# Six recurrence levels as 64x64 products on two output halves, gathered in a 512-column table

## The reference

```python
def hgrn2_recurrence(q, k, v, logf):       # 4 heads, key and value width 128
    n = T // CHUNK                          # CHUNK = 64, so 4 chunks
    def step(S, blk):
        G = jnp.cumsum(gc, axis=-2)
        decay = jnp.exp(jnp.where(causal, G[t] - G[s], MASK_VALUE))
        scores = jnp.einsum('bhtd,bhsd,bhtsd->bhts', qc, kc, decay)
        o = scores @ vc + (qc * jnp.exp(G)) @ S
        S = S * jnp.exp(G_end) + (kc * jnp.exp(G_end - G)).T @ vc
        ...
```

## Time and profile before

| | |
|---|---|
| median of three runs | 796.02 us (795.48 to 796.18) |
| profiled execution | 795.0 us, of which the span of the instructions is 793.2 us |
| PE busy | 784.6 us, 99% |
| DVE busy | 585.7 us, 74% |
| ACT busy | 479.5 us, 60% |
| POOL busy | 28.0 us, 4% |
| DMA | 149.55 MB, mean 189 GB/s |

### The profile page before, as it was taken

How to read it: one execution, slowest core, us unless ns; L and a number is a source line. 1 busy time by engine, 2 the same in 40 slices (tenths; PEclk the granted TensorE clock), 3 DMA queues, 4 the chain that set the end, 5 groups by cost and what they waited for, 6 DMA issues and landing times.

```text
span 793.2 us, 11382 instructions
## 1 busy us (share of the span) xinstructions
PE 784.6 (99%) x4440; PEld 672.9 (85%) x4440; DVE 585.7 (74%) x682; ACT 479.5 (60%) x582; POOL 28.0 (4%) x63
## 2 busy tenths in 40 slices
PE   8999999999999999999999999999999999999998
PEld 8988888888998987888888998888888888888877
DVE  7799885576678888557558678458589878686883
ACT  6875487544676558653467654444477666665682
POOL 8100000000000000300000000000000000000000
PEclk9999999999999999999999999999999999999999
DMA  8555344465436624456636435664049979797921
GB/s 273 187 180 163 127 137 159 160 212 177 142 115 204 196 86 145 138 197 193 209 113 206 161 108 170 204 208 159 1 153 344 370 281 336 264 324 257 348 83 53
DMA packets 70037, 149.55 MB, mean 189 GB/s; under 512 B 8458, under 2 KB 11104, under 8 KB 69984
## 3 DMA queue, kind: packets, MB, share of 16 engines
q1 hardware_dynamic: 69568, 148.78, 55.4%
q0 software_dynamic: 384, 0.04, 0.2%
q10 hardware_dynamic: 32, 0.01, 0.0%
HBM read 147.76 MB, written 1.05 MB: 188 GB/s over the span
## 4 chain that ended last, share of the span: by engine, by line
PE 89%; DVE 4%; ACT 3%; DMA 2%; issue 1%; SPq 1%; POOL 0%; POOLq 0%; DVEq 0%; ACTq 0%
PE mm L613 16%; PE mm L615 16%; PE mm L614 16%; PE aux L1107 5%; PE aux L1109 5%; PE aux L1108 5%; PE mm L629 3%; PE mm L630 3%; PE mm L631 3%; PE aux L721 3%; PE aux L835 2%; DMA sb_raw<-in_w_in 2%; PE aux L613 1%; PE aux L615 1%; PE aux L614 1%
## 5 line engine op out<-in xcount | busy, mean ns | idle before, releaser
L1691 DVE TENSOR_TENSOR sb_w_lo<-sb_raw,sb_w_hi 128x2048 fp32r<-128x2048 f32 (+2 forms) x153 | 319.4, 2097 | 74.2 <-ACT sb_w_hi L1223 40.7
L1223 ACT ACTIVATE sb_w_hi<-sb_raw 128x2048 fp32r<-128x2048 f32 (+1 forms) x83 | 155.1, 1871 | 118.3 <-PE mm L615 87.6
L613 PE MATMUL mm<-sb_w_hi,sb_hT_hi 128*128 128x512 f32 (+1 forms) x456 | 175.8, 386 | 0.6 <-DVE sb_w_lo L1691 0.5
L615 PE MATMUL mm<-sb_w_hi,sb_hT_lo 128*128 128x512 f32 (+1 forms) x456 | 172.6, 379 | 0.0
L614 PE MATMUL mm<-sb_w_lo,sb_hT_hi 128*128 128x512 f32 (+1 forms) x456 | 172.6, 379 | 0.0
L1539 ACT ACTIVATE sb_w_hi<-sb_raw 128x2048 fp32r<-128x2048 f32 x50 | 95.6, 1917 | 35.7 <-PE aux L1109 17.7
L613 PEld LDWEIGHTS mm<-sb_w_hi,sb_hT_hi 128*128 128x128 f32 x456 | 85.8, 188 | 18.2 <-issue 2.8
L615 PEld LDWEIGHTS mm<-sb_w_hi,sb_hT_lo 128*128 128x128 f32 x456 | 85.8, 188 | 16.2
L614 PEld LDWEIGHTS mm<-sb_w_lo,sb_hT_hi 128*128 128x128 f32 x456 | 85.9, 188 | 15.0
L629 PE MATMUL mm<-sb_hT_hi,sb_w_hi 128*128 128x256 f32 x272 | 78.2, 288 | 0.0
L630 PE MATMUL mm<-sb_hT_lo,sb_w_hi 128*128 128x256 f32 x272 | 76.9, 283 | 0.0
(11 more groups left out here) (395 smaller groups left out, 1183.2 us busy)
## 6 DMA issues: line engine op xcount, KB each, us to landing
sb_raw<-in_w_in SPq DMA_DIRECT2D x120, 512.0 KB, 4.6
sb_raw<-in_w_down SPq DMA_DIRECT2D x32, 512.0 KB, 5.4
sb_raw<-in_w_gate SPq DMA_DIRECT2D x31, 512.0 KB, 4.7
sb_raw<-in_w_up SPq DMA_DIRECT2D x31, 512.0 KB, 6.1
sb_raw<-in_w_out SPq DMA_DIRECT2D x16, 512.0 KB, 4.1
sb_raw<-in_w_up_attn SPq DMA_DIRECT2D x8, 512.0 KB, 4.6
sb_raw<-in_w_up_hgrn SPq DMA_DIRECT2D x8, 512.0 KB, 4.0
sb_raw<-in_w_o SPq DMA_DIRECT2D x8, 512.0 KB, 4.1
```

What stands on the lines that cost most here:

```text
L613: pe.matmul(dst, a_hi, rhs[0], start=start, stop=False, skip_group_check=True)
L615: return pe.matmul(dst, a_lo, rhs[0], start=False, stop=stop, skip_group_check=True)
L1223: act.activation(w_hi[:, slot(t), 0:width], raw[:, slot(t), 0:width], ACT.Copy).then_inc(hi_split, 1)
L1691: return dve.tensor_tensor(out_, a, b, op)
```

## The change

The pair level and levels 2 to 6 have groups of at most 64 tokens. So each block of 128 tokens is now cut in two stretches of 64. For each of the eight blocks, TensorE does two products with 64 columns of weights and 64 moving columns over all 128 rows: one for the lower half, whose output goes to PSUM partitions 0 to 63, and one for the upper half, whose output goes to partitions 64 to 127, both in the same 64 columns. The 96 products of 128x128x128 become 192 of 128x64x64, the halves in turn.

The result of a level is 128 x 512 and not 128 x 1024. `take_level` gathers it with masks of 64 columns in a new table `near` of 512 columns. When level 6 is in, ScalarE copies `near` to the two diagonal quadrants of each block of `acc` in two instructions of 64 partitions x 512 columns (`spread_near`, in step 15 behind `level_exp(8)` and ahead of `exps(2)`). TensorE's `hgrn_out` waits for both of them too, and in the second layer VectorE's first `take_level` waits for the first layer's copies. Level 7, level 8 and the rest stay. In the setup there are six masks of 128x64 in place of seven of 128x128, and one more table of 512 columns is filled with zeros.

```diff
-N_MASKS = len(LEVELS) - 1
+N_MASKS = len(LEVELS) - 2
...
-        lmask = sb("lmask", [P, len(LEVELS) - 1, P], U8)
+        lmask = sb("lmask", [P, N_MASKS, 64], U8)
+        near = sb("near", [P, 512])
...
                         a, b = (fT, logf) if j == "pair" else (e, e)
                         for i in range(8):
-                            last = pe.matmul(ps[:, i * P:(i + 1) * P], a[:, i * P:(i + 1) * P], b[:, i * P:(i + 1) * P],
-                                             start=True, stop=True)
+                            for h in range(2):
+                                block = slice(i * P + 64 * h, i * P + 64 * h + 64)
+                                last = pe.matmul(ps[64 * h:64 * h + 64, i * 64:(i + 1) * 64], a[:, block], b[:, block],
+                                                 start=True, stop=True, skip_group_check=True)
...
                 def hgrn_out():
                     pe.wait_ge(S["acc_ready"], L + 1)
+                    pe.wait_ge(S["near_spread"], 2 * L + 2)
...
+                def spread_near():
+
+                    act.wait_ge(S["near_ready"], L + 1)
+                    for h in range(2):
+                        rows_ = slice(64 * h, 64 * h + 64)
+                        act.activation(acc[rows_, :].rearrange("p (i t) -> p i t", i=8)[:, :, rows_],
+                                       near[rows_, :].rearrange("p (i t) -> p i t", i=8), ACT.Copy).then_inc(S["near_spread"], 1)
...
-                    15: [lambda: level_exp(8), lambda: exps(2, L, 4), lambda: sink_exp(2, 4)],
+                    15: [lambda: level_exp(8), spread_near, lambda: exps(2, L, 4), lambda: sink_exp(2, 4)],
...
-                for i, j in enumerate(LEVELS[:-1]):
+                for i, j in enumerate(LEVELS[:-2]):
                     size = 1 if j == "pair" else 1 << (j - 1)
-                    ins = dve.tensor_scalar(begins_i[:, i:i + 1], iota_s[:, i:i + 1], -size, None, ALU.bitwise_and)
+                    ins = dve.tensor_scalar(begins_i[:, i:i + 1], iota_s[:, i:i + 1], 64 - size, None, ALU.bitwise_and)
...
-                    ins = ts_(lmask[:, i, :], iota_f, begins[:, i:i + 1], ALU.is_ge)
+                    ins = ts_(lmask[:, i, :], iota_f[:, 0:64], begins[:, i:i + 1], ALU.is_ge)
...
             link(dve.memset(acc[:], 0.0))
+            link(dve.memset(near[:], 0.0))
...
-                    ins = dve.copy_predicated(acc[:, :].rearrange("p (i t) -> p i t", i=8),
-                                              lmask[:, LEVELS.index(j):LEVELS.index(j) + 1, :].broadcast_to([P, 8, P]),
-                                              aux[pair][:, :].rearrange("p (i t) -> p i t", i=8))
-                    release(ins, aux_free[pair], value)
+                    if j == "pair" and L == 1:
+                        dve.wait_ge(S["near_spread"], 2)
+                    ins = dve.copy_predicated(near[:, :].rearrange("p (i t) -> p i t", i=8),
+                                              lmask[:, LEVELS.index(j):LEVELS.index(j) + 1, :].broadcast_to([P, 8, 64]),
+                                              aux[pair][:, 0:W].rearrange("p (i t) -> p i t", i=8))
+                    release(ins, aux_free[pair], value, S["near_ready"] if j == 6 else None)
```

More of the change, by code:

```diff
@@ L368, in build @@
                  "fT_ready", "sig_ready", "log_ready", "kTh_ready", "qTh_ready",
-                 "vh_ready", "D_ready", "k_taken", "q_taken", "E_ready", "W_ready", "acc_ready", "sc128_ready",
+                 "vh_ready", "D_ready", "k_taken", "q_taken", "E_ready", "W_ready", "acc_ready", "near_ready", "near_spread", "sc128_ready",
                  "qk_ready", "v_ready", "qT_ready", "kT_ready", "S_ready", "p_ready", "p_normed", "z_scaled", "sinkexp_in",
```

## The result

The changed kernel takes 787.79 us, the median of four runs (787.30 to 788.18). The kernel before, run beside it, took 795.75 us (795.45 to 796.18). The profiled execution took 787.45 us (span 785.7 us) against 795.0 us: 7.55 us less.

The account below looks back on a forecast made before the run. TensorE's list of work, busy 99% of the span, was taken to bound the kernel. Savings of 2.83 and 4.08 us took 6.9 off 795.0, giving 788.1; 1.0 more for the median made 789.1 us, range 787.9 to 792.0.

Parts of the forecast that it names:

- The saving between the levels and the experts: Both layers' levels, pair to 6: shorter products and masked copies save 2.83 and 4.08 us, 6.9 us together.
- Blocks of products: TensorE, levels pair to 6: two halves go as one, so a block takes 1.42 us where it took 2.02.
- the change of width: TensorE, going to half-width products: 0.09 us added ahead of each new block, between 0 and 0.11 at level 5.
- Rival A: TensorE's levels: halves run in turn, a block grows to 2.35 us, kernel slower at 797.9 us; chance 0.07.
- Masked copy: VectorE, 12 copies: 512 columns take 0.74 us where 1024 took 1.325, 0.585 us less each.
- Levels 3 to 6: First layer: 0.97, 0.70, 0.65 and 0.51 us saved, sum 2.83; second layer, with pair and level 2, 4.08.
- Rival B: VectorE: the masked copy does not get shorter, so only 4.4 us are saved, 791.6 us; chance 0.12.
- Spread: ScalarE's two copies, at most 2.0 us, fit its 2.47 us idle before the third attention unit's exponentials: no cost.
- Rival C, the clock: First layer, after pair and level 2: idle TensorE falls to 1.2 GHz for 3 us stretches; about 792 us; chance 0.05.
- 0 saved: First layer, pair: the next tile waits for VectorE's low part until 49.79 us, so shorter products gain nothing there.
- Nothing is given back: From 82 us on no TensorE product waits for VectorE, so none of the saving is lost later: 0 us.
- the median of three lies 1.0 above it: Last step, whole kernel: 1.0 us added to the profiled execution's 788.1, giving 789.1 us.

Follow-up runs that it names:

- experiment 5: Changed kernel with each level's eight lower-half products issued first, then all eight upper ones, instead of alternating: 794.86 us.
- experiments 3: Changed kernel with every masked copy on VectorE done twice in a row, products still in halves: 791.92 us.
- number 4: Changed kernel with the old 128x128x128 products, masked copies taking only the first 64 columns of each block: 793.57 us.
- experiment 6: Changed kernel without ScalarE's two `spread_near` copies and the two waits for them: 788.26 us.
- Experiment 7: Changed kernel with ScalarE's copy of `sb_pT` one step sooner, ahead of the third attention unit's exponentials: 787.39 us.

## Why the prediction was off, step by step

**The saving between the levels and the experts: right, in mechanism and size.** 6.9 us was forecast and 7.0 measured in the stretch. The rest of this section says where the parts of it came out otherwise, and why the time was missed all the same.

**Blocks of products: right.** 1.42 us was forecast for a free block and 1.42 measured; the change of width was put at 0.09 us and is 0.09 (0.32 against 0.23). That both halves go in one slot was inferred from line 794, and experiment 5 shows how narrowly it holds: it needs the halves in turn. Rival A's price of a pass was right, its block 0.18 us too long. The Trainium skill ("TensorE: Matmul & The Clock Gate", on packing small matmuls) lets a weight load overlap only with another row group; here both halves use all rows and the pairs overlap, so the measurement decides.

**Masked copy: right.** 0.740 us for 0.74; the fixed part and the proportion taken from two other vector operations carried over.

**Levels 3 to 6: right.** 2.89 us in the first layer where 2.83 was forecast. In the second, 4.17 where 4.08 was; the order in which pair and level 2 give their part differs (PE gains 0.54 us at once, and 0.76 at tile 8), the sum 1.30 is as forecast. Together 7.06 for 6.91 us. Both parts were needed, and experiments 3 and 4 give the split. Rival B falls with the copies' 0.740 us.

**Spread: right.** It costs nothing (experiment 6).

**Rival C, the clock: did not come.** TensorE waited 0.23 us behind level pair and 1.12 behind level 2 of the first layer, and the granted clock is 1.00 (2.4 GHz) both from 44 to 62 and from 62 to 130 us. No run shows a stretch at half speed there, so the 3 us of the forecast stayed an assumption.

**"0 saved" at pair in the first layer: wrong by 0.2 to 0.4 us.** DVE's lateness was read from one execution in which it was larger than in the next (2.08 against 1.70 us from the block to tile 7), because TensorE had started earlier in it.

**"Nothing is given back": wrong by 0.5 us.** The working asked who waits for DVE after 82 us in the trace of before, and found no one. The question was how much each of TensorE's operands is ahead by. TensorE came 3.2 us earlier (its last pass before line 795 at 118.27 and not 121.50), the copy of `sb_pT` only 2.1 us (120.76 to 118.66), and the 1.06 us of reserve was used up. Experiment 7 shows the place. Why the copy gains only 2.1 us was read from the traces: ScalarE's work is 2.03 us earlier from the first unit's exponentials on (87.53 to 85.50 us), which was TensorE's lead when it came to the first scores (2.06 us behind level 4), and it stays so; levels 5 and 6, behind those scores, gave 1.2 us to TensorE alone.

**Experts' stage: not foreseen, -0.5 us.** ScalarE starts on the first expert tile when the second of its four pieces has landed. In the kernel before that piece, issued at 584.12 us, lands after 5.0 us. While it is on its way one packet of queue q8, kind instruction, is under way too, and the fourth issue of SP takes 2.13 us (585.11). The first piece of `w_up` in the DMA view (window 584.13 to 584.40 us; the last number is the time to its landing), then queue q8 in the window 585.0 to 587.1 us, then PE:

```profile
sb_raw<-in_w_up SPq DMA_DIRECT2D x1, 256.0 KB, 5.0
```

```profile
q8 instruction: 1, 0.02, 5.9%
```

```profile
590.68 0.47 PE L1107 MATMUL aux<-sb_w_hi,sb_hT_hi 128*128 128x512 f32 x1 [1.00 <-DVE sb_w_lo L1691]
```

In the changed kernel the same piece, issued at 577.23 us, lands after 3.7 us, the fourth issue takes 0.38 us, no packet of q8 lies beside them, and PE starts without a wait (window 577.24 to 577.50 us, then PE):

```profile
sb_raw<-in_w_up SPq DMA_DIRECT2D x1, 256.0 KB, 3.7
```

```profile
582.58 0.47 PE L1111 MATMUL aux<-sb_w_hi,sb_hT_hi 128*128 128x512 f32 x1
```

The second trace of the kernel before has the packet too, the piece lands after 4.9 us and the fourth issue takes 2.03. All other edited versions gain here as well. In number 5 TensorE comes to this stage 1.0 us later than in the first trace of before; no packet lies beside the piece, it lands after 3.8 us, and TensorE still gains 1.2 us. In number 4 a packet begins 0.7 us later relative to the work than before and is half as long (0.97 against 1.97 us); the piece lands after 4.1 us and the gain is 0.8. So the 1.2 us go with that packet and not with the levels being faster. That the packet causes the late landing is argued from these ten traces and not tested, and so is why it falls elsewhere in the edited versions. Of the 1.2 us, 0.6 to 0.7 go again 15 to 21 us later in the two traces of the changed kernel, but only 0 to 0.3 in those of the other edited versions; the cause of that is open.

**The failed step is the last one: "the median of three lies 1.0 above it".** That term measured 0.34 us for the changed kernel. The sum was right for the profiled execution to 0.65 us (788.1 against 787.45). Then 1.0 us was added because the one profiled run was 1.0 below the median of three. But that is the spread of single runs, not a property of the kernel: 26 later runs of the kernel before lie between 794.45 and 796.44, their medians 795.42 and 795.3, and 796.02 was the highest median of all. The changed kernel's profiled run is 0.34 below its median, and in its second set 0.24 (788.07 against 788.31). With 795.4 for the kernel before, 6.9 off gives 788.5; 787.8 and 788.3 were measured. Either half of the miss alone would have stayed inside the range. Of the 1.3 us between forecast and result, 0.65 is this anchor and the rest the small steps above: -0.4 at the start, +0.5 at line 795, -0.5 in the experts, -0.15 in the levels, -0.1 behind the experts' stage.

**The range** held the unknown costs of the change and nothing for the median of few runs, which had moved by 0.6 us between sets of the same kernel. Its low end, 1.2 us under the forecast, was cut to the slot of level 7 alone, while the steps called 0 had room only to the good side. The saving of 6.9 us itself lies inside both measured intervals (6.7 to 9.4 us, and 5.9 to 8.5).

## What to carry to other kernels

When a change shortens one engine's list, go through that engine's later operands and write down by how much each is early; the smallest reserve, not the lack of a wait, says what is given back. When a change has two parts, price each alone in the stretch of the trace where it works: here 2.4 and 3.2 us made 7.0, and most of what seemed to be missing was that the control had made one part dearer than it had been. And when the forecast is a small difference, take the time before as the middle of everything measured, and give the range the spread of the runs in both directions.

## What the runs showed of the hardware

Two passes with 64 weight columns each, all 128 rows and outputs on opposite partition halves go through in one slot of 0.062 us on average if they alternate (1.15 us less 0.22, over 15). If eight blocks of one half come before the other, each pass starts 0.058 us behind the one before, except for three at the seam between the halves, which start beside another. Alternation is worth 0.75 of the block's 1.90 us.

Where a packet of queue q8, kind instruction, is under way beside the first expert tile, its second piece lands after 5.0 and 4.9 us and an issue of SP's takes 2.13 and 2.03 us; without it 3.7 to 3.9 us and 0.38 us. TensorE is 1.2 us later for it. That the one causes the other is not tested.

The start of the program varies between executions of the same kernel. Windows of 5 to 7 us, the first trace of the kernel before and the second:

```profile
5.00:7.00 2.00, 2.00 (x18) 1.97 (x19) 1.27 (x7) 0.23 (x1) 2.00 (x5) 1.00 1.03 312
```

```profile
5.00:7.00 2.00, 2.00 (x12) 1.74 (x12) 1.28 (x7) 0.00 (x0) 2.00 (x5) 1.00 1.00 314
```

The same four passes of 128x128x128, a moment later in the second trace:

```profile
5.08 0.71 PE L802 MATMUL aux<-sb_ident 128*128 128x128 f32 x4
```

```profile
5.53 1.16 PE L802 MATMUL aux<-sb_ident 128*128 128x128 f32 x4
```

PE is busy throughout in both windows and the row says granted clock 1.00 for both, yet one has 18 matmuls and the other 12. The passes' starts tell more: away from the small product of line 807, passes follow each other by 0.21 us up to 4.3 us in the first trace and up to 6.5 in the second, and by 0.11 us behind that. That is half the pace and then the full one, as between 1.2 and 2.4 GHz. The trace's own record of the clock begins only at 4.43 and at 6.50 us, with 1.00, so the row says nothing of the time before. In the ten traces of this case that moment lies between 4.43 and 7.62 us, and level pair starts up to 1.6 us later where it is late. TensorE had been at work since 1.61 us in both; why the moment differs is open.

The first weight product follows 0.9 us apart (9.38 and 10.28 us), of which 0.4 us reach the end (795.0 and 795.39 us), because tile 7 waits less in the later one. The changed kernel's two traces differ in the same way (18 and 11 matmuls; 4.90 and 6.61 us). It is as large as the steps that this forecast argued about.
